# A recurrent mixer's first two output blocks taken one token tile at a time, with the low weights by halves and the second slab's low weights last

## What is computed

```python
# end of layer 0
h = layer_norm(ALPHA * h + sq_relu_mlp(h, mlp_w1[0], mlp_w2[0]), ln_g[0, 1], ln_b[0, 1])
# layer 1, rglru_mixer(h, ...): w_in is 1024 x 2560
gate_branch, rec = jnp.split(x @ w_in, 2, axis=-1)
gate_branch = jax.nn.gelu(gate_branch)
u = conv(rec, conv_w, width 4, causal) + conv_b            # per channel, along the tokens
r = sigmoid(u_blocks @ w_a + b_a);  i = sigmoid(u_blocks @ w_x + b_x)
a = exp(-8 * r * softplus(-lam));   b_in = sqrt(-expm1(2 * log_a)) * (i * u)
h = scan(h_t = a_t * h_{t-1} + b_in_t)
out = (h * gate_branch) @ w_o
```

## Time and profile before

| | |
|---|---|
| runs | 1968.51 us median of 3 (1968.50 to 1968.57) |
| the profiled execution | 1970.6 us, of which the span of instructions is 1968.8 us |
| busy in the span | PE 1943.3, weight loads 1757.5, DVE 1383.1, ACT 927.8 us |
| PE idle before line 1185 at 391.68 us | 0.91 us |
| PE idle before line 1420 at 394.37 us | 0.67 us |
| PE idle before line 1054 at 459.86 us | 2.09 us |

### The profile page before, as it was taken

How to read it: one execution, slowest core, us unless ns; L and a number is a source line. 1 busy time by engine, 2 the same in 40 slices (tenths; PEclk the granted TensorE clock), 3 DMA queues, 4 the chain that set the end, 5 groups by cost and what they waited for, 6 DMA issues and landing times.

```text
span 1968.8 us, 30115 instructions
## 1 busy us (share of the span) xinstructions
PE 1943.3 (99%) x12844; PEld 1757.5 (89%) x12844; DVE 1383.1 (70%) x1405; ACT 927.8 (47%) x883; POOL 22.5 (1%) x45
## 2 busy tenths in 40 slices
PE   8999999999999999999999999999999999999998
PEld 7989899897988888888998898889998998999997
DVE  7776866688865787756867686577666557667666
ACT  5454443378433374343345443344445555654444
POOL 0000000000000000000000000000000010000000
PEclk9999999999999999999999999999999999999999
DMA  9435545444655344544634465544557564344552
GB/s 347 173 134 194 207 175 209 171 170 157 235 191 193 147 153 170 227 180 171 235 140 181 150 246 188 196 150 166 192 190 253 183 159 163 129 171 161 192 192 107
DMA packets 32283, 361.80 MB, mean 184 GB/s; under 512 B 3837, under 2 KB 4354, under 8 KB 10034
## 3 DMA queue, kind: packets, MB, share of 16 engines
q1 hardware_dynamic: 28434, 347.49, 47.8%
q0 software_dynamic: 3744, 12.77, 2.6%
HBM read 359.15 MB, written 1.10 MB: 183 GB/s over the span
## 4 chain that ended last, share of the span: by engine, by line
PE 94%; DVE 3%; ACT 2%; issue 1%; DMA 0%; SPq 0%; DVEq 0%; ACTq 0%
PE acc L1042 27%; PE bank L956 12%; PE bank L916 5%; PE bank L918 5%; PE bank L917 5%; PE bank L1726 4%; PE bank L953 4%; PE bank L1857 3%; PE acc L1054 2%; PE bank L1204 2%; PE acc L1071 1%; PE bank L969 1%; PE bank L971 1%; PE bank L970 1%; PE acc L918 1%; PE acc L916 1%
## 5 line engine op out<-in xcount | busy, mean ns | idle before, releaser
L2831 DVE TENSOR_TENSOR w_lo<-raw,w_hi 128x4096 fp32r<-128x4096 f32 (+3 forms) x82 | 307.8, 3754 | 108.9 <-ACT w_hi L2175 108.9
L2164 ACT ACTIVATE w_hi<-raw 128x2048 fp32r<-128x2048 f32 x173 | 323.1, 1910 | 62.4 <-PE bank L918 38.5
L2175 ACT ACTIVATE w_hi<-raw 128x4096 fp32r<-128x4096 f32 (+3 forms) x87 | 269.4, 3096 | 161.9 <-PE bank L1726 151.0
L2826 DVE TENSOR_TENSOR w_lo<-raw,w_hi 128x2048 fp32r<-128x2048 f32 x98 | 220.1, 2288 | 77.2 <-ACT w_hi L2164 77.2
L956 PEld LDWEIGHTS bank<-ht_both,w_hi 128*128 128x128 f32 x2112 | 247.1, 188 | 4.4
L956 PE MATMUL bank<-ht_both,w_hi 128*128 128x256 f32 x2112 | 247.8, 276 | 0.0
L916 PE MATMUL bank<-ht_both,w_hi 128*128 128x256 f32 x704 | 196.1, 278 | 0.0
L918 PE MATMUL bank<-ht_both,w_lo 128*128 128x256 f32 x704 | 195.6, 278 | 0.0
L917 PE MATMUL bank<-ht_both,w_hi 128*128 128x256 f32 x704 | 195.6, 278 | 0.0
L1042 PE MATMUL acc<-w_hi,mlp_hi 128*128 128x512 f32 x448 | 143.9, 391 | 0.0
L1042 PE MATMUL acc<-w_lo,mlp_hi 128*128 128x512 f32 x448 | 143.3, 389 | 0.0
(11 more groups left out here) (560 smaller groups left out, 3765.2 us busy)
## 6 DMA issues: line engine op xcount, KB each, us to landing
raw<-slabs_in SPq DMA_DIRECT2D x147, 2048.0 KB, 7.7
raw<-slabs_in SPq DMA_DIRECT2D x23, 1024.0 KB, 6.8
raw<-slabs_in SPq DMA_DIRECT2D x12, 512.0 KB, 10.9
g_tab<-gains_in POOLq DMA_DIRECT2D x11, 512.0 KB, 6.3
b_tab<-gains_in POOLq DMA_DIRECT2D x8, 512.0 KB, 9.4
raw<-slabs_in SPq DMA_DIRECT2D x2, 1152.0 KB, 5.7
raw<-slabs_in SPq DMA_DIRECT2D x1, 1280.0 KB, 5.7
a_bias<-bias_rows POOLq DMA_DIRECT2D x8, 128.5 KB, 3.4
```

The costliest lines, as they stand in the source:

```text
L2164: nc.scalar.activation(w_hi[g][:, c], raw[g][:, c], ACT.Copy)\
L2175: nc.scalar.activation(w_hi[g][:, 0:w], raw[g][:, 0:w], ACT.Copy).then_inc(hi_ready, 1)
L2826: ins = nc.vector.tensor_tensor(w_lo[g][:, c], raw[g][:, c], w_hi[g][:, c].bitcast(F32), ALU.subtract)
L2831: nc.vector.tensor_tensor(w_lo[g][:, 0:w], raw[g][:, 0:w], w_hi[g][:, 0:w].bitcast(F32), ALU.subtract).then_inc(lo_ready, 1)
```

## The change

- Layer 0's `down_end` gets `ahead=first_blocks_tile(0)`: the 64 high products of blocks 0 and 1 for token tile 0. Each former 256-column matmul is now two of 128 columns, one for each token tile, so `first_blocks_tile(0)` and `(1)` together issue 128 matmuls in place of 64. The four `keep_clock` go.
- `first_blocks_low` then does the 32 low products over all 256 tokens, in two halves of k; slab g0 joins `AHEAD_NORMS`, by which DVE signals the first half of `w_lo` separately (`ahead_lo`).
- Slab g0+1 goes through `branch_low_last` in place of `branch`.
- `ht_part` of tile 0's second half moves ahead of tile 1's second residual addition, and the transposes of tile 1 take the banks acc00 and acc01.

```diff
@@ take / AHEAD
-            take_transposes(2 * layer + 2, aligned=layer == DEPTH - 1, ahead=layer > 0)
+            take_transposes(2 * layer + 2, aligned=layer == DEPTH - 1, ahead=True)
-        AHEAD_NORMS = (0, 2, 3, 4, 5, 6, N_LN + 1)
+        AHEAD_NORMS = (0, 1, 2, 3, 4, 5, 6, N_LN + 1)
@@ new functions of PE
+            def first_blocks_tile(t):
+                g, c = FIRST["mix", 1], slice(t * P, (t + 1) * P)
+                if t == 0:
+                    pe.wait_ge(hi_ready, g + 1)
+                    for i in range(2):
+                        wait_free("lin", i)
+                for half in range(2):
+                    for i in range(2):
+                        for j in range(2):
+                            for k in range(4 * half, 4 * half + 4):
+                                need_ht(k, [t])
+                                a = k * 512 + i * 256 + j * P
+                                o = psum("lin", i)[:, j * S + t * P:j * S + (t + 1) * P]
+                                for x in (ht_hi, ht_lo):
+                                    nc.tensor.matmul(o, w_hi[g][:, a:a + P], x[:, k, c],
+                                                     start=t == 0 and j == 0 and k == 0 and x is ht_hi, stop=False)
+            def first_blocks_low():
+                g = FIRST["mix", 1]
+                for half in range(2):
+                    pe.wait_ge(*((ahead_lo, AHEAD[g]) if half == 0 else (lo_ready, g + 1)))
+                    for i in range(2):
+                        for j in range(2):
+                            for k in range(4 * half, 4 * half + 4):
+                                a = k * 512 + i * 256 + j * P
+                                m = nc.tensor.matmul(psum("lin", i)[:, j * S:(j + 1) * S], w_lo[g][:, a:a + P],
+                                                     ht_hi[:, k, :], start=False, stop=j == 1 and k == KD - 1)
+                        if half == 1:
+                            m.then_inc(bank_full[ticket["lin", i][0]], 1)
@@ lru of PE
                 def branch_low_last(s):
-                    g = g0 + s + 1
+                    g = g0 + s + (s > 2)
-                for i in range(2):
-                    wait_free("lin", i)
-                pe.wait_ge(hi_ready, g0 + 1)
-                block_high(g0, 0, range(2), range(KD))
-                block_high(g0, 1, range(1), range(KD))
-                need(g0)
-                block_low(g0, 0)
-                block_high(g0, 1, range(1, 2), range(KD))
-                block_low(g0, 1)
-                for s in range(1, 3):
-                    branch(s)
+                first_blocks_tile(1)
+                first_blocks_low()
+                branch_low_last(1)
+                branch(2)
@@ mlp of PE
-                         ahead=(lambda: mixer_ahead(layer + 1)) if layer in (1, 2)
+                         ahead=(lambda: first_blocks_tile(0)) if layer == 0
+                         else (lambda: mixer_ahead(layer + 1)) if layer in (1, 2)
@@ norm_tile of DVE
                             ht_part(early, t - 1, 0)
-                            if n != 1:
-                                ht_part(early, t - 1, 1)
+                            ht_part(early, t - 1, 1)
```

## The result

| | before | after |
|---|---|---|
| median | 1969.15 us (22 runs, 1968.15 to 1973.16) | 1972.70 us (22 runs, 1970.94 to 1979.78) |
| profiled execution, its span | 1970.6, 1968.8 us | 1971.06, 1969.3 us |

The ratio is 1.0018, 95% interval [1.0012, 1.0023]: 3.5 us slower. That is just under the 0.2% that the prediction took as its bound for a difference that can be told; over 22 runs each the interval does exclude 1. The forecast was 1970.8, 2.3 us over before, and "no change that can be told, on the slow side".

A forecast was written before the change was run, and what follows sets the result against it. Bound: the moment block 5 is full, which starts ACT and DVE. Sum: +1.9 (blocks 0 and 1) - 0.4 (rate) + 0.65 (wait) + 0.1 = +2.3 us on the median 1968.51, so 1970.8; range 1967.0 to 1973.2.

The forecast's parts named there:

- Step 1: Price of a 128-column matmul on PE: 0.111 us from matmul to matmul, limited by the weight load.
- Rival 1: Narrow matmuls cost by columns, 0.06 us each; block 5 full at 427.0, 1.5 us faster, 1967.0; 10%.
- Rival 4: A narrow fp32r matmul is slower than a wide one, 0.22 us: +14 us more, 1984.9; 4%.
- Step 2: Blocks 0 and 1 on PE: late transposes, an idle time of some 1.1 us before tile 1, PE 1.9 us later.
- Step 3: DVE behind the late `ht_part`: convolutions 3.8 us later, `w_lo` of g0+2 ready at 419.4.
- Step 4: Slabs g0+1, g0+2: low last costs 0, 0.65 us wait before `branch(2)`, block 5 full at 430.8, sum +2.3 us.
- The 0.4 us put down to a faster rate up to g0+2: 256-column matmuls behind the narrow ones, up to g0+2: 0.1134 us each, taking 0.4 us off the sum.
- Step 5: Behind block 5: everything moves by 2.3 us, convolution 9 stays hidden; 1970.8 us in all.
- DVE's cover: At convolution 9: DVE ends at 432.1, ACT asks at 434.1, so 2 us of cover hide DVE's lateness.
- my own case: The forecast by steps: 1970.8 us, range 1970.0 to 1971.8; chance 58%.
- rival 3: DVE's convolutions lose 2 us more and the cover is gone: +3.5 to +5, 1972.0 to 1973.5; 13%.
- whether falls would vanish: PE's clock falls near 460.4 and 491.2, 1.5 us each: 1969.3 with one gone, 1967.8 with both; 15%.

The follow-up runs named there:

- e6: The kernel before with only slab g0+1 taken low last; 1970.58 us, ratio 0.9998 to the kernel before.
- e12: The changed kernel once more, unedited (also spelled e12_same); 1972.77 us, ratio 1.0018 to the kernel before.
- e3: The changed kernel with slab g0+2 taken low last too; 1975.56 us, ratio 1.0033 to the kernel before.
- e10: The changed kernel with slab g0+2 low last too, run a second time (e3's kernel); 1973.54 us, ratio 1.0020 to the kernel before.
- e11: e10's kernel with one 512-column matmul on constants in the idle time before tile 1; 1975.19 us, ratio 1.0023 to the kernel before.
- e4: The changed kernel with one matmul on constants in the idle time before tile 1's narrow matmuls; 1973.02 us, ratio 1.0014 to the kernel before.
- e5: The kernel before with one 512-column matmul, its result overwritten, ahead of block 0; 1970.93 us, ratio 1.0006 to the kernel before.
- e7: The changed kernel with only block 0 by token tiles, block 1's high products 256 columns wide behind tile 1; 1969.76 us, ratio 0.9995 to before.
- e2_noahead: The changed kernel with matmuls on constants instead of work ahead, blocks 0 and 1 then 256 columns wide; 1971.99 us, ratio 1.0006 to before.

## Why the prediction was right

**Step 1, the narrow matmul: right.** 0.111 to 0.113 measured, 0.111 forecast from the 192-column rows. Rival 1 (0.06, or the 81 ns of the Trainium skill, "TensorE: Matmul & The Clock Gate", section "Back-to-back issue gap") is out for fp32r operands here. The rule for weight loads of the Trainium skill (same page, section "LDWEIGHTS (loading the stationary operand)"; worked out for 128 columns an estimate of 107 ns) is 4 to 5% under the measured spacing. Rival 4 is out as well.

**Step 2, blocks 0 and 1: right.** Transposes at 7.09 for 7.1, tile 1 at 9.13 for 9.1, idle time 0.97 for 1.1. Tile 1 and the lows took 7.20 and 3.70 us for 7.1 and 3.63, so all of it ended 0.2 us later than forecast.

**Step 3, DVE: right in mechanism,** its first convolution 0.3 us later than forecast (4.1 for 3.8), 0.2 of it PE's.

**Step 4: right, and the low-last order of g0+1 costs nothing** (e6). The wait before `branch(2)` was 0.64 us for 0.65. The 0.4 us put down to a faster rate up to g0+2 came out in after and e12, but not in e3, e10 and e11, whose code up to there is the same but for e11's one matmul: that term was right by luck of the execution. The mis-sized terms: that 0.3 of DVE arrives here, and the slab g0+2 took 43.38 - 31.72 = 11.66 us from its first matmul to ACT's copy, of which 0.2 was not in my sum. Together +2.8 for +2.3. In e12, at 0.113 in this slab, the same distance gives +2.4: the half microsecond is within what one kernel does from one execution to the next.

**Step 5: right.** w_o moved by the same 2.8 as block 5, with DVE's cover still there.

**The whole time: +3.5 for +2.3.** The forecast of 1970.8 stood on a median of 1968.51 from 3 runs; over 22 it is 1969.15, which is 0.6 of the 1.9 us between forecast and result. 1972.70 lies outside the range that I gave my own case, 1970.0 to 1971.8, and inside the whole range thanks to its width. It also lies among rival 3's numbers (1972.0 to 1973.5), but rival 3 is not what happened: the convolutions came 0.3 us later than forecast, not 2, and the cover of step 5 held.

Of after's 22 runs the 18 at a clock of 0.997 or more have a mean of 1972.33, against 1969.65 for the 22 of before: +2.7, the local number. All 22 have 1973.41: the four others add 1.1. In the median they show by 0.2 only; the 18 alone have a median 3.3 over before's, mostly because before's median lies 0.5 under its mean. **Here the prediction lacked a rival.** It asked of the clock only whether falls would vanish, and priced a vanished one by its length. In fact the two that after's profile lacks were worth 0.3 and 0.56 us instead of 1.5 each, the first because ACT limits that stretch; and a new one, four times as long and in a stretch that PE limits, costs 6.4. Shown are this fall, its place and its price (e10), and that the changed kernel has runs at 0.996 where before has none. That filling the idle time takes them away is likely (e4, e11); what makes such a run come in one execution and not in the next stays open.

What also stays open is what sets 0.113 or 0.118 for 256 columns. And no version here is shown to beat before in whole time: e5 and e7 are 1.0 us ahead of before at block 5 and w_o, which the faster rate of their profiled executions can account for, and stand at 1.0006 and 0.9995, both with 1 in their intervals. DVE's w_lo of g0+2 put earlier under the faster rate was not seen.

## What to carry to other kernels

Before splitting a matmul into narrower ones to start sooner, look at the nearest narrow rows: if the spacing no longer falls with the columns, the split doubles the cost of what it moves, and only as much of it is free as fits into the existing idle time (here 32 matmuls, not 64). A price of a clock fall or of a wait holds only where PE sets the end of the stretch; read first what PE would wait for if it were faster. And an edit can bring new falls of the clock in some executions only, with an idle time hardly longer than the former ones (0.97 against 0.91 us): look at more than one execution, and at the mean clock of each.

## What had not been expected of the hardware

- A fall of the granted clock of 13.65 us (397.42 to 411.07 in e10), where those of the earlier trace rows and of e2_noahead lasted 3.4. It was seen in this one profile; a mean clock of 0.996 or less, which fits it, came in 12 of 52 executions of the kernels with the idle time of 0.97 us followed by narrow matmuls.
- Matmuls of 256 columns run at either 0.113 or 0.118 us for a whole stream, in the 14 profiles here, and change only behind a stop. The same code has had both: g0+2 at 0.118 in after and at 0.113 in e12_same. Over layer 1's first three slabs it is worth up to 288 x 0.0045 = 1.3 us.
- A fall of 3.4 us was worth 0.3 us up to the next boundary where PE waits for ACT behind it, and such falls come and go between executions of one kernel (after without, e12_same with).
